# A table of parameters, gated opening loads, later spreads and a smaller GpSimd share in a hybrid decoder layer

## The chip, the core and the metric

The kernel runs on one core of a Trainium2 chip. The metric is the device time of one execution in microseconds (us). The engines named below are TensorE (PE, with its weight loads shown apart as PEld), VectorE (DVE), ScalarE (ACT), GpSimd (POOL) and SyncE (SP), whose queue issues all the transfers between HBM and the on-chip memory. The engines run side by side and wait for one another by semaphores.

## The reference

One layer of a decoder runs on 1024 prompt tokens and 8 sample tokens, 1032 columns in all, with a model width of 1024:

```python
h = rmsnorm(x, g_mix)
q, f, i, g, u = split(h @ w_in)              # 5 x 512 columns
y_a = hgrn2(silu(q), f, i) normed per head * hgrn_norm * sigmoid(g)
y_b = (pooled(u) @ pool_mix) * pool_scale    # windows 2, 4, 8, 16
x = x + concat(y_a, y_b) @ w_out
x = x + cross_attend(rmsnorm(x, g_cross), k, v, w_cq, w_co)   # k, v from rmsnorm(mem, g_mem) @ w_kv
x = x + (silu(a) * b) @ w_ffn_out            # a, b = split(rmsnorm(x, g_ffn) @ w_ffn_in)
y = rmsnorm(x, g_final)
```

It returns y, the recurrent states, the last pooling rows and the memory's keys and values, all in float32.

## The kernel before

Activations lie transposed, channels on the 128 partitions and the 1032 columns in three thirds of 344 (CH). Each float32 operand is split in a rounded high part and a low part, and a product is three matmuls per 128 rows of depth: high by high, low by high, high by low. A weight matrix is taken in stripes of 128 output channels, held in two slots. A stripe goes through SP's load into `raw`, ACT's rounding into `w_hi`, DVE's difference into `w_lo`, and then through three chunks on PE, one per third, each of 8 x 3 matmuls of 344 columns.

The opening is written out by hand. SP issues, in order, `g_mix` (L542), the first two stripes (L540), the nine parts of x that PE uses (L548; three parts a third, of 3, 3 and 2 of the 8 blocks of depth), and the nine blocks of token rows `xt` from which the norms are summed (L552), with stripe 2 behind the third and stripe 3 behind the last. Six small parameters follow (L557 to L567): the gains of the other norms, the bounds, `hgrn_norm` and `pool_scale`, each gathered in single elements. Only then stripes 4 and 5 are issued, and the states.

ACT rounds the first stripe in `first_hi(0)` (L1098, eight instructions), half of the second, three parts of x in `x_round` (L1112), the other half, and the remaining six parts. Then it squares the token rows (`x_square`, L1107) and makes the norm's factors of a third (`x_factors`). DVE makes the low parts: `first_lo(0)` (L1559), three times `x_rest` (L1552), `first_lo(1)`, six times `x_rest`. POOL makes constants first. PE waits for the ninth of them, runs seven warm-up products of 128 x 512 (L2293, `WARM`), and then `first_chunk` 0 to 5, which alternate between stripe 0 and stripe 1 over the thirds 0, 1 and 2. The second part of a chunk's x is needed at its fourth block of depth, the third part at its seventh.

The norm of x is applied when a chunk leaves PSUM. PE spreads the factors of a third over all partitions (`spread_rows`, L2269): third 0 after chunk 4, third 1 after chunk 5, third 2 after the first chunk of stripe 2. DVE copies the spread rows (L1566) and only then empties the chunks (`first_evac`, L1572; `plain_evac`, L1612).

Much later, at the mixer's end, y is gated (`gate`, L1757) and split. For the second third POOL makes four low parts (L901), DVE gates the last third, makes its four low parts (`rest_a`, L1798) and those of the pooled half (`rest_b`, L1804). PE enters the product with `w_out` and waits for these parts in `y_ready`.

Of the kernel before, what the change touches and what calls it, by code (L numbers as in the profile page):

```python
# [88 lines left out]
def hybrid_layer(nc, t):  # L89
# [9 lines left out]
    with ExitStack() as ctx:  # L99
# [29 lines left out]
        gains = put("gains", [P, 3, KB])  # L129
        gmem = put("gmem", [P, KB])  # L130
        lbt = put("lbt", [P, 2, H])
        lbw = put("lbw", [P, 4, H])
        omlb = put("omlb", [P, H])
        hnorm = put("hnorm", [P, H])
        pscale = put("pscale", [P, H])
# [126 lines left out]
        WARM = 7  # L262
# [18 lines left out]
        const_in = sem("const_in")  # L281
        gmix_in = sem("gmix_in")
# [238 lines left out]
        def _(sp):  # L521
            def load_stripe(p, i, s, wait=True):
# [19 lines left out]
            sp.dma_start(gains[:, 0, :], t["g_mix"].rearrange("(k p) -> p k", p=P),  # L542
                         allow_slow_non_contiguous=True).then_inc(gmix_in, 16)
# [12 lines left out]
            load_stripe(phases[0], 1, 1)  # L556
            sp.dma_start(gains[:, 1, :], t["g_cross"].rearrange("(k p) -> p k", p=P),  # L557
                         allow_slow_non_contiguous=True).then_inc(const_in, 16)
            sp.dma_start(gains[:, 2, :], t["g_ffn"].rearrange("(k p) -> p k", p=P),
                         allow_slow_non_contiguous=True).then_inc(const_in, 16)  # L560
            sp.dma_start(gmem[:, :], t["g_mem"].rearrange("(k p) -> p k", p=P),
                         allow_slow_non_contiguous=True).then_inc(const_in, 16)
            sp.dma_start(lbt[:, :, :], t["hgrn_lb"].rearrange("l (h p) -> p l h", p=P),
                         allow_slow_non_contiguous=True).then_inc(const_in, 16)
            sp.dma_start(hnorm[:, :], t["hgrn_norm"].rearrange("(h p) -> p h", p=P),
                         allow_slow_non_contiguous=True).then_inc(const_in, 16)
            sp.dma_start(pscale[:, :], t["pool_scale"].rearrange("(h p) -> p h", p=P),  # L567
                         allow_slow_non_contiguous=True).then_inc(const_in, 16)
# [231 lines left out]
        def _(pool):  # L800
# [87 lines left out]
            def mixer_end():  # L888
# [10 lines left out]
                for h in range(H):  # L899
# [118 lines left out]
            for p in phases:  # L1018
# [24 lines left out]
                if p is phases[0]:  # L1043
                    pool.wait_ge(gmix_in, 16)
# [30 lines left out]
        def _(act):  # L1075
# [17 lines left out]
            def first_hi(s, k0=0, k1=KB):  # L1093

                act.wait_ge(gmix_in, 16)
                act.wait_ge(raw_in[s], 16)
                for k in range(k0, k1):
                    last = act.activation(w_hi[s][:, k, :], raw[:, s, k, :], ACT.Copy, scale=gains[:, 0, k:k + 1])  # L1098
                if k1 == KB:
                    last.then_inc(hi_made, 1)  # L1100
# [431 lines left out]
        def _(dve):  # L1532
# [22 lines left out]
            def first_lo(s):  # L1555

                dve.wait_ge(hi_made, s + 1)
                for k in range(KB):
                    last = dve.scalar_tensor_tensor(w_lo[s][:, k, :], raw[:, s, k, :], gains[:, 0, k:k + 1],  # L1559
                                                    w_hi[s][:, k, :].bitcast(F32), ALU.mult, ALU.subtract)  # L1560
                last.then_inc(lo_made, 1)
# [681 lines left out]
        def _(pe):  # L2243
# [552 lines left out]
```

## Time and profile before

| | us |
|---|---|
| median of 3 runs | 1426.41 |
| lowest and highest | 1426.29, 1426.75 |
| the profiled execution, its own time | 1426.6 |
| its span, first to last instruction | 1424.8 |

The profiled execution spends 1.8 us outside its span. PE is busy for 1405.1 us of it. DVE is busy for 886.4, POOL for 576.4 and ACT for 420.5 us, so that PE is the engine whose idle time counts.

### The profile page before, as it was taken

Reading aid. Unit: us, or ns where it says so; the run is one execution under the profiler, and the core shown is the slowest. Engines: PE = TensorE matmul, PEld = TensorE weight load, DVE = VectorE, ACT = ScalarE, POOL = GpSimd, SP = SyncE. Lnnn points to the kernel's source line nnn. Section 1 sums busy time; section 2 is a strip of 40 time slices with the busy share of each in tenths; the row PEclk is TensorE's granted clock in tenths of the full one; section 3 lists DMA queues with packets and bytes.
Section 4 is the critical chain, followed back from the end, with each engine's and each line's share of the span. In section 5 each row is a group of like instructions: output and inputs, shape, how many; then the busy total and the mean of one; then the engine's idle time right before and its main releaser. Section 6 shows DMA issues by size and latency. Waiting matters only on the chain.

```text
span 1424.8 us, 25495 instructions
## 1 busy us (share of the span) xinstructions
PE 1405.1 (99%) x9965; PEld 1364.1 (96%) x9965; DVE 886.4 (62%) x1350; ACT 420.5 (30%) x632; POOL 576.4 (40%) x457
## 2 busy tenths in 40 slices
PE   9999999999999999999999999999999999999997
PEld 7999999989999988799999999999999999999996
DVE  4425677878754257757995676676667658633335
ACT  6131435370021136510052222323222222311111
POOL 1231246135532010134663787778777610000163
PEclk9999999999999999999999999999999999999999
DMA  9412211101162275611132222222222142523113
GB/s 297 127 45 67 68 31 38 38 23 46 50 185 61 74 251 173 212 45 45 44 89 75 76 74 89 74 70 78 89 74 67 54 155 74 173 93 109 33 45 119
DMA packets 163567, 129.19 MB, mean 91 GB/s; under 512 B 11532, under 2 KB 148748, under 8 KB 163363
## 3 DMA queue, kind: packets, MB, share of 16 engines
q1 hardware_dynamic: 163499, 128.25, 29.0%
q8 instruction: 47, 0.77, 0.2%
q14 instruction: 21, 0.17, 0.0%
HBM read 107.88 MB, written 20.58 MB: 90 GB/s over the span
## 4 chain that ended last, share of the span: by engine, by line
PE 67%; POOL 13%; issue 10%; DVE 7%; ACT 2%; POOLq 0%; DVEq 0%; ACTq 0%
PE pm L2249 17%; PE pm L2251 17%; PE pm L2250 17%; POOL raw L981 3%; POOL gb L999 3%; POOL raw_c L981 2%; POOL sum L988 2%; POOL sum L986 2%; PE pm L2520 2%; PE pm L2522 2%; PE pm L2521 2%; POOL raw_c L993 1%; POOL raw L993 1%; DVE xf L1826 1%; PE pm L2293 1%
## 5 line engine op out<-in xcount | busy, mean ns | idle before, releaser
L2249 PE MATMUL pm<-x_hi,w_hi 128*128 128x344 f32 x960 | 310.5, 323 | 0.6 <-DVE gb L1612 0.6
L2251 PE MATMUL pm<-x_hi,w_lo 128*128 128x344 f32 x960 | 306.6, 319 | 0.0
L2250 PE MATMUL pm<-x_lo,w_hi 128*128 128x344 f32 x960 | 306.6, 319 | 0.0
L1084 ACT ACTIVATE w_hi<-raw 128x1024 fp32r<-128x1024 f32 x88 | 93.3, 1060 | 530.2 <-PE pm L2251 444.7
L2249 PEld LDWEIGHTS pm<-x_hi,w_hi 128*128 128x128 f32 x960 | 180.5, 188 | 2.5 <-issue 1.8
L2250 PEld LDWEIGHTS pm<-x_lo,w_hi 128*128 128x128 f32 x960 | 180.4, 188 | 0.2
L2251 PEld LDWEIGHTS pm<-x_hi,w_lo 128*128 128x128 f32 x960 | 180.4, 188 | 0.0
L1545 DVE TENSOR_TENSOR w_lo<-raw,w_hi 128x1024 fp32r<-128x1024 f32 x79 | 113.8, 1441 | 9.7 <-ACT w_hi L1084 9.7
L831 POOL TENSOR_TENSOR raw<-raw,gains 128x1024 f32<-128x1024 f32 x32 | 64.7, 2025 | 127.4 <-DMA raw<-in_w_in 81.0
L2096 DVE TENSOR_TENSOR gb<-gb,ga 128x1032 f32<-128x1032 f32 x19 | 53.0, 2789 | 89.9 <-POOL gb L999 89.9
L2207 DVE TENSOR_TENSOR acc<-pm,acc 128x344 f32<-128x344 f32 x66 | 33.9, 516 | 112.1 <-PE pm L2251 112.0
L913 POOL TENSOR_TENSOR fp<-acc 128x344 f32 (+1 forms) x22 | 21.3, 967 | 201.8 <-DVE acc L2207 196.9
L998 POOL TENSOR_TENSOR ga<-ga,rb 128x1032 f32<-128x1032 f32 x19 | 52.6, 2769 | 85.9 <-DVE ga L2112 85.9
L2520 PE MATMUL pm<-x_hi,w_hi 128*128 128x258 f32 x304 | 86.6, 285 | 0.3
L2521 PE MATMUL pm<-tl,wh 128*128 128x258 f32 x304 | 85.9, 283 | 0.0
L2522 PE MATMUL pm<-th,wl 128*128 128x258 f32 x304 | 85.9, 282 | 0.0
L2520 PE MATMUL pm<-th,wh 128*128 128x258 f32 x304 | 85.8, 282 | 0.0
L2521 PE MATMUL pm<-tl,w_hi 128*128 128x258 f32 x304 | 85.8, 282 | 0.0
L2522 PE MATMUL pm<-x_hi,w_lo 128*128 128x258 f32 x304 | 85.7, 282 | 0.0
L2521 PE MATMUL pm<-x_lo,w_hi 128*128 128x258 f32 x304 | 85.7, 282 | 0.0
L2522 PE MATMUL pm<-th,w_lo 128*128 128x258 f32 x304 | 85.6, 282 | 0.0
L2520 PE MATMUL pm<-th,w_hi 128*128 128x258 f32 x304 | 85.6, 281 | 0.0
(366 smaller groups left out, 3972.9 us busy)
## 6 DMA issues: line engine op xcount, KB each, us to landing
raw<-in_w_ffn_in SPq DMA_DIRECT2D x24, 512.0 KB, 4.5
sg_raw<-s_rows SPq DMA_DIRECT2D x22, 516.0 KB, 5.0
s_rows<-gb SPq DMA_DIRECT2D x21, 516.0 KB, 2.7
raw<-in_w_in SPq DMA_DIRECT2D x20, 512.0 KB, 3.8
raw_c<-in_w_ffn_in SPq DMA_DIRECT2D x20, 512.0 KB, 5.0
sk<-in_cache_k_cols SPq DMA_DIRECT2D x16, 512.0 KB, 6.9
raw<-in_w_out SPq DMA_DIRECT2D x8, 512.0 KB, 3.6
raw<-in_w_cq SPq DMA_DIRECT2D x8, 512.0 KB, 3.6
```

The costliest lines, as they stand in the source:

```text
L831: pool.tensor_tensor(raw[:, s, :, :], raw[:, s, :, :], g, ALU.mult).then_inc(gain_on, 1)
L981: pool.tensor_tensor(r[:, s, :, :], r[:, s, :, :], g, ALU.mult).then_inc(gain7_on, 1)
L998: pool.tensor_tensor(ga[:, :], ga[:, :], rb[:, :], ALU.mult).then_inc(row_scaled, 1)
L1084: act.activation(w_hi[s][:, :, :], src, ACT.Copy).then_inc(hi_made, 1)
L1545: dve.tensor_tensor(w_lo[s][:, :, :], raw[:, s, :, :], w_hi[s][:, :, :].bitcast(F32), ALU.subtract).then_inc(lo_made, 1)
L2096: dve.tensor_tensor(gb[par][:, :], gb[par][:, :], ga[:, :], ALU.mult).then_inc(row_made, 1)
L2249: pe.matmul(out, w_hi[s][:, k, :], hi[:, k, x0:x0 + cols], start=(k == 0), stop=False)
L2250: pe.matmul(out, w_hi[s][:, k, :], lo[:, k, x0:x0 + cols], start=False, stop=False)
L2251: last = pe.matmul(out, w_lo[s][:, k, :], hi[:, k, x0:x0 + cols], start=False, stop=(k == kb - 1))
L2520: pe.matmul(out, wh7[n][:, j, :], hi(j, c), start=j == 0, stop=False)
L2521: pe.matmul(out, wh7[n][:, j, :], lo(j, c), start=False, stop=False)
L2522: last = pe.matmul(out, wl7[n][:, j, :], hi(j, c), start=False, stop=j == KP - 1)
```

## The change

It has five parts.

1. The seven small parameters are packed on the host into one array of 128 x 48 and loaded with one DMA into `table`, of which `gains`, `gmem`, `lbt`, `hnorm` and `pscale` become views. It takes the place of `g_mix` at the head of SP's queue.
2. Stripe 0 is loaded in two halves. SP holds the parts of x, stripe 1 and five of the blocks of token rows back until an earlier load has landed. Stripe 1 moves behind the third part of x and waits for the first part.
3. ACT and DVE make both stripes in halves, and PE starts its first chunk when the first half of stripe 0 and the first part of x are ready. ACT rounds the first half of stripe 1 ahead of the third part of x.
4. The warm-up becomes 20 products of 128 x 128 and waits for the third constant instead of the ninth. The spreads of the thirds 1 and 2 move one chunk later on PE, and ACT rounds stripe 2 ahead of three squares.
5. At the mixer's end POOL makes two of the four low parts of the second third, and DVE the other two ahead of its last gate.

```diff
-            sp.dma_start(gains[:, 0, :], t["g_mix"]...).then_inc(gmix_in, 16)
-            load_stripe(phases[0], 0, 0, False)
-            load_stripe(phases[0], 0, 1, False)
+            first_w = t["w_in"].rearrange("(k p) n -> p k n", p=P)[:, :, 4 * P:5 * P]
+            sp.dma_start(table[:, :], t["table"]).then_inc(table_in, 16)
+            sp.dma_start(raw[:, 0, 0:KP, :], first_w[:, 0:KP, :]).then_inc(first_in, 16)
+            sp.dma_start(raw[:, 0, KP:KB, :], first_w[:, KP:KB, :]).then_inc(raw_in[0], 16)
             for n in range(9):
                 c, (k0, k1) = n // 3, PARTS[n % 3]
+                if n == 1:
+                    sp.wait_ge(first_in, 16)
+                if n == 2:
+                    sp.wait_ge(raw_in[0], 16)
+                if n in (4, 5, 7, 8):
+                    sp.wait_ge(x_in[n - 3 if n < 6 else n - 4], 16)
+                if n == 6:
+                    sp.wait_ge(raw_in[1], 16)
                 sp.dma_start(xc[:, c, k0:k1, :], t["x_cols"][c, :, k0:k1, :]).then_inc(x_in[n], 16)
+                if n == 2:
+                    sp.wait_ge(x_in[0], 16)
+                    load_stripe(phases[0], 0, 1, False)
             for n in range(9):
...
+                if n < 3:
+                    sp.wait_ge(x_in[5 + n], 16)
+                if n == 4:
+                    sp.wait_ge(xt_in[0], 48)
+                if n == 7:
+                    sp.wait_ge(xt_in[1], 48)
                 sp.dma_start(xt[n][0:own, :], t["x_prompt"][0, t0:t0 + own, :]).then_inc(xt_in[n // 3], 16)
...
-            (six loads of small parameters)
...
-            first_hi(0)
-            first_hi(1, 0, KB // 2)
-            for n in range(3):
-                x_round(n)
-            first_hi(1, KB // 2, KB)
+            first_hi(0, 0, KP)
+            first_hi(0, KP, KB)
+            x_round(0)
+            x_round(1)
+            first_hi(1, 0, KP)
+            x_round(2)
+            first_hi(1, KP, KB)
...
             x_factors(0)
+            split_hi(phases[0], 1, 0, phases[0].done + 5)
             for n in range(3, 6):
                 x_square(n)
-            split_hi(phases[0], 1, 0, phases[0].done + 5)
...
-            pe.wait_ge(setup, 9)
+            pe.wait_ge(setup, 3)
             for _ in range(WARM):
-                pe.matmul(bank[7][:, :], ones[:, :], keep[:, :], start=True, stop=True)
+                pe.matmul(bank[7][:, 0:P], ones[:, :], ones[:, :], start=True, stop=True)
             for q in range(6):
                 first_chunk(q)
-                if q in (4, 5):
-                    spread_rows(q - 4)
+                if q == 4:
+                    spread_rows(0)
...
                 stripe_chunk(ph["qfi"], 1, 0, c, x_hi, x_lo)
-                if c == 0:
-                    spread_rows(2)
+                if c < 2:
+                    spread_rows(c + 1)
...
-                for h in range(H):
+                for h in range(2):
                     pool.wait_ge(yhi2_made, h + 1)
...
                 rest_b(1)
+                rest_a(1, 2)
                 gate(2)
-                rest_a(2)
+                rest_a(2, 0)
```

On SP, at the head of the program, these rows stood before, `xc` the parts of x and `raw` a stripe:

```order
1 L542 DMA gains<-in_g_mix 128x8x1
2 L540 DMA raw<-in_w_in 128x8x128 x2
3 L548 DMA xc<-in_x_cols 128x1032 x2
4 L548 DMA xc<-in_x_cols 128x688
5 L548 DMA xc<-in_x_cols 128x1032 x2
```

and these stand there now, with their waits (`first_in`, `raw_in0` and `raw_in1` are the halves of stripe 0 and stripe 1, `load_in0` and on the parts of x):

```order
1 L545 DMA table<-in_table 128x48
2 L546 DMA raw<-in_w_in 128x4x128
3 L547 DMA raw<-in_w_in 128x4x128
4 L558 DMA xc<-in_x_cols 128x1032
5 L558 DMA xc<-in_x_cols 128x1032 [waits first_in]
6 L558 DMA xc<-in_x_cols 128x688 [waits raw_in0]
7 L542 DMA raw<-in_w_in 128x8x128 [waits load_in0]
8 L558 DMA xc<-in_x_cols 128x1032
9 L558 DMA xc<-in_x_cols 128x1032 [waits load_in1]
```

Stripe 1 has moved from the third place in the queue to the seventh, and is issued after x's first part has landed.

On ACT, in the same stretch, before (`w_hi_52` is stripe 0, `w_hi_53` stripe 1):

```order
2 L1098 ACTIVATE w_hi_52<-raw,gains 128x128 x8
3 L1098 ACTIVATE w_hi_53<-raw,gains 128x128 x4
4 L1112 ACTIVATE x_hi<-xc 128x3x344 x2
5 L1112 ACTIVATE x_hi<-xc 128x2x344
6 L1098 ACTIVATE w_hi_53<-raw,gains 128x128 x4
```

and now:

```order
2 L1105 ACTIVATE w_hi_52<-raw,table 128x128 x8
3 L1118 ACTIVATE x_hi<-xc 128x3x344 x2
4 L1105 ACTIVATE w_hi_53<-raw,table 128x128 x4
5 L1118 ACTIVATE x_hi<-xc 128x2x344
6 L1105 ACTIVATE w_hi_53<-raw,table 128x128 x4
```

The first half of stripe 1 now stands between the second and the third part of x.

On DVE at the mixer's end, before:

```order
241 L1804 SCALAR_TENSOR_TENSOR y_lo<-pm,pscale,y_hi 128x344 [waits yb_hi] x4
242 L1757 TENSOR_TENSOR proj<-proj 128x344 [waits o_scaled,g_act]
243 L1757 TENSOR_TENSOR proj<-proj 128x344 [waits o_scaled] x3
244 L1798 TENSOR_TENSOR y_lo<-proj,y_hi 128x344 [waits yhi2_made] x4
245 L1804 SCALAR_TENSOR_TENSOR y_lo<-pm,pscale,y_hi 128x344 [waits yb_hi] x4
```

and now:

```order
245 L1815 SCALAR_TENSOR_TENSOR y_lo<-pm,table,y_hi 128x344 [waits yb_hi] x4
246 L1809 TENSOR_TENSOR y_lo<-proj,y_hi 128x344 [waits yhi2_made] x2
247 L1768 TENSOR_TENSOR proj<-proj 128x344 [waits o_scaled,g_act]
248 L1768 TENSOR_TENSOR proj<-proj 128x344 [waits o_scaled] x3
249 L1809 TENSOR_TENSOR y_lo<-proj,y_hi 128x344 [waits yhi2_made] x4
250 L1815 SCALAR_TENSOR_TENSOR y_lo<-pm,table,y_hi 128x344 [waits yb_hi] x4
```

Row 246 is new: two low parts of the second third stand ahead of the last third's gate.

## Rows read from the trace of the kernel before

**Rows 1.** The page, busy time: us, share of the span, instructions.

```profile
PE 1405.1 (99%) x9965; PEld 1364.1 (96%) x9965; DVE 886.4 (62%) x1350; ACT 420.5 (30%) x632; POOL 576.4 (40%) x457
```

**Rows 2.** Waits of PE, whole span: us in total, times, longest.

```profile
PE pm L2293 <- POOL eps L818: 3.4, 1, 3.4
PE pm L2355 <- DVE e L1682: 1.4, 1, 1.4
```

**Rows 3.** Timeline of PE and its weight loads, opening: start, us, what.

```profile
3.44 8.76 PE L2293 MATMUL pm<-keep,ones 128*128 128x512 f32 x14 [3.44 <-POOL eps L818]
11.82 0.54 PE L2283 MATMUL pm<-x_hi,w_hi 128*128 128x344 f32 x1
15.88 0.42 PE L2283 MATMUL pm<-x_hi,w_hi 128*128 128x344 f32 x1
7.87 0.34 PEld L2293 LDWEIGHTS pm<-keep,ones 128*128 128x128 f32 x1 [0.52 <-issue]
8.61 0.19 PEld L2293 LDWEIGHTS pm<-keep,ones 128*128 128x128 f32 x1 [0.40 <-issue]
```

**Rows 4.** Timeline of ACT, opening.

```profile
5.53 3.61 ACT L1098 ACTIVATE w_hi<-raw,gains 128x128 fp32r<-128x128 f32 x12 [3.43 <-DMA raw<-in_w_in]
10.61 1.73 ACT L1112 ACTIVATE x_hi<-xc 128x1032 fp32r<-128x1032 f32 x2 [0.20 <-DMA xc<-in_x_cols]
```

**Rows 5.** Timeline of DVE, opening.

```profile
10.44 3.28 DVE L1552 TENSOR_TENSOR x_lo<-xc,x_hi 128x1032 fp32r<-128x1032 f32 x3 [0.24 <-ACT x_hi L1112]
13.64 2.18 DVE L1559 SCALAR_TENSOR_TENSOR w_lo<-raw,gains,w_hi 128x128 fp32r<-128x128 f32 x8
```

**Rows 6.** Timeline of SP's queue: when it issued what.

```profile
1.30 1.19 SPq L540 DMA_DIRECT2D raw<-in_w_in  x2
2.53 5.47 SPq L548 DMA_DIRECT2D xc<-in_x_cols  x9
```

**Rows 7.** DMA issues in windows at 1.3, 1.95, 2.55 and 45: us to landing last.

```profile
raw<-in_w_in SPq DMA_DIRECT2D x1, 512.0 KB, 4.1
raw<-in_w_in SPq DMA_DIRECT2D x1, 512.0 KB, 5.2
xc<-in_x_cols SPq DMA_DIRECT2D x1, 516.0 KB, 6.8
raw<-in_w_in SPq DMA_DIRECT2D x1, 512.0 KB, 3.8
```

**Rows 8.** Timeline of PE and DVE and ACT around the third spread.

```profile
39.43 0.21 ACT L1119 ACTIVATE rtok<-rtok 128x3 f32<-128x3 f32 x1
40.32 0.80 PE L2269 MATMUL pm<-ident,rtok 128*128 128x128 f32 x6
41.15 0.52 DVE L1566 COPY rb<-pm 128x344 f32<-128x344 f32 x1 [3.13 <-PE pm L2269]
42.98 2.44 DVE L1545 TENSOR_TENSOR w_lo<-raw,w_hi 128x1024 fp32r<-128x1024 f32 x1
35.15 1.23 DVE L1545 TENSOR_TENSOR w_lo<-raw,w_hi 128x1024 fp32r<-128x1024 f32 x1 [1.76 <-ACT w_hi L1084]
```

**Rows 9.** Timeline at the mixer's end: DVE, POOL, PE.

```profile
312.80 3.23 DVE L1757 TENSOR_TENSOR proj<-proj 128x344 f32<-128x344 f32 x4
317.66 2.01 DVE L1804 SCALAR_TENSOR_TENSOR y_lo<-pm,pscale,y_hi 128x344 fp32r<-128x344 f32 x4
311.09 4.14 POOL L901 TENSOR_TENSOR y_lo<-proj,y_hi 128x344 fp32r<-128x344 f32 x4 [8.20 <-ACT y_hi L1250]
315.33 0.40 PE L2249 MATMUL pm<-y_hi,w_hi 128*128 128x344 f32 x1 [0.24 <-issue]
319.73 0.42 PE L2249 MATMUL pm<-y_hi,w_hi 128*128 128x344 f32 x1 [0.38 <-DVE y_lo L1804]
302.45 2.10 DVE L1757 TENSOR_TENSOR proj<-proj 128x344 f32<-128x344 f32 x4
315.95 1.79 DVE L1798 TENSOR_TENSOR y_lo<-proj,y_hi 128x344 fp32r<-128x344 f32 x4
```

More of the change, by code:

```diff
@@ L128, in hybrid_layer @@
         rb = put("rb", [P, T])
-        gains = put("gains", [P, 3, KB])
-        gmem = put("gmem", [P, KB])
-        lbt = put("lbt", [P, 2, H])
+        table = put("table", [P, 48])
+        gains = table[:, 0:3 * KB].rearrange("p (n k) -> p n k", n=3)
+        gmem = table[:, 24:32]
+        lbt = table[:, 32:40].rearrange("p (n h) -> p n h", n=2)
+        hnorm, pscale = table[:, 40:44], table[:, 44:48]
         lbw = put("lbw", [P, 4, H])
         omlb = put("omlb", [P, H])
-        hnorm = put("hnorm", [P, H])
-        pscale = put("pscale", [P, H])
         ss = put("ss", [P, 16])
@@ L1093, in first_hi @@
             def first_hi(s, k0=0, k1=KB):
-                act.wait_ge(gmix_in, 16)
-                act.wait_ge(raw_in[s], 16)
+                act.wait_ge(table_in, 16)
+                act.wait_ge(*((first_in, 16) if (s, k0) == (0, 0) else (raw_in[s], 16)))
                 for k in range(k0, k1):
                     last = act.activation(w_hi[s][:, k, :], raw[:, s, k, :], ACT.Copy, scale=gains[:, 0, k:k + 1])
-                if k1 == KB:
-                    last.then_inc(hi_made, 1)
+                last.then_inc(*((hi_made, 1) if k1 == KB else (first_halves, 1)))
             def x_square(n):
@@ L1553, in x_rest, with first_lo @@
                                   ALU.subtract).then_inc(x_split, 1)
-            def first_lo(s):
-                dve.wait_ge(hi_made, s + 1)
-                for k in range(KB):
+            def first_lo(s, k0, k1):
+                dve.wait_ge(table_in, 16)
+                dve.wait_ge(*((hi_made, s + 1) if k1 == KB else (first_halves, s + 1)))
+                for k in range(k0, k1):
                     last = dve.scalar_tensor_tensor(w_lo[s][:, k, :], raw[:, s, k, :], gains[:, 0, k:k + 1],
                                                     w_hi[s][:, k, :].bitcast(F32), ALU.mult, ALU.subtract)
-                last.then_inc(lo_made, 1)
+                last.then_inc(*((lo_made, 1) if k1 == KB else (first_rests, 1)))
             def spread_factors(c):
@@ L1794, in mixer_end, with rest_a @@
             def mixer_end():
-                def rest_a(c):
-                    for h in range(H):
+                def rest_a(c, h0):
+                    for h in range(h0, H):
                         dve.wait_ge(yhi2_made, H * (c - 1) + h + 1)
@@ L2275, in first_chunk @@
                 s, c = FIRST_CHUNKS[q]
-                pe.wait_ge(lo_made, s + 1)
+                pe.wait_ge(*((first_rests, s + 1) if c == 0 else (lo_made, s + 1)))
                 out, at = bank[q][:, 0:CH], slice(c * CH, (c + 1) * CH)
@@ L2471, in y_ready @@
                 pe.wait_ge(yb_made, H * (c + 1))
-                pe.wait_ge(*((ya2_made, H) if c == 2 else (ya_made, H * (c + 1))))
+                if c < 2:
+                    pe.wait_ge(ya_made, (H, H + 2)[c])
+                if c:
+                    pe.wait_ge(ya2_made, (None, 2, 2 + H)[c])
             def norm_sums(n):
@@ L2788 @@
     t["cache_k_cols"] = nc.dram_tensor("in_cache_k_cols", a.shape, mybir.dt.from_np(a.dtype), kind="ExternalInput").ap()
+    g = [inputs[n].reshape(KB, P).T for n in ("g_mix", "g_cross", "g_ffn", "g_mem")]
+    g += [inputs[n].reshape(-1, P).T for n in ("hgrn_lb", "hgrn_norm", "pool_scale")]
+    arrays["in_table"] = a = np.ascontiguousarray(np.concatenate(g, axis=1))
+    t["table"] = nc.dram_tensor("in_table", a.shape, mybir.dt.from_np(a.dtype), kind="ExternalInput").ap()
     t["s_rows"] = nc.dram_tensor("s_rows", (P, FB, T), F32).ap()
```

34 lines of the change are left out of this document (13 added, 21 removed).

## The prediction

> **What bounds the kernel now.** I read the busy times first. PE works for 1405.1 of the span's 1424.8 us [rows 1], so the kernel gains only where PE stands idle or does work that computes nothing, and loses where an edit makes PE wait. The list of PE's waits shows where that is: 3.4 us before its first warm-up product, 1.4 us in the recurrence and little else [rows 2]. The timeline of the opening shows the large piece. PE starts at 3.44 us with seven warm-up products, 14 records of 8.76 us in all, and its first useful matmul starts at 11.82 us [rows 3]. All 11.8 us are without use, and from then on PE has hardly a gap: the second chunk starts at 15.88 [rows 3], as DVE's low part of stripe 1, 2.18 us from 13.64 on, ends [rows 5].
>
> Who holds the first matmul? ACT rounds stripe 0 and half of stripe 1 in 3.61 us from 5.53 on [rows 4]. Then it waits for the first part of x, which SP issued at 2.53 [rows 6] and which landed 6.8 us later, at 9.3 [rows 7]. With 1.06 us of rounding and one of DVE's three parts, begun at 10.44, x is ready about 11.5 [rows 5], and the warm-up ends at 11.6 or so. Both end together.
>
> **The opening, step by step.** Times are from the span's start, with before's durations.
>
> The table takes g_mix's place, and stripe 0 is issued at 1.3 us as before. Its first half is half the bytes of a load that took 4.1 us from issue [rows 7]. I take 4.3 for its landing and 5.2 for the whole stripe. ACT's eight rounding instructions take 0.3 us each (3.61 for twelve, [rows 4]), so they run from 4.4 to 6.8. DVE's take 0.27 us each (2.18 for eight, [rows 5]), and its second half ends at 7.9.
>
> The first part of x is now the second half megabyte in the queue. In the trace before that was stripe 1, issued at 1.9 and landed after 5.2 us, at 7.1 [rows 6, 7]. I take 6.8 for x. Its rounding ends at 7.9 and its low part at 9.0. The first useful matmul can start at 9.1, some 2.7 us sooner, if the warm-up is over.
>
> The warm-up starts when POOL's third constant is set, between 0 and the 3.4 us at which before's nine and two more were there [rows 2]; I take 1.8. Forty passes of 128 columns by the fast level of the trace, some 0.13 us each (0.80 for six, [rows 8]), would be over at 7; by twice that they would be over at 12.4. The level changes on the way: the weight loads of the old warm-up took 0.34 us up to 7.87 and 0.19 from 8.61 on, 1.2 GHz and then 2.4 [rows 3], some 5 us after PE began. With 5 us of the slow level from 1.8 on, that is 19 passes, and 21 fast ones in 2.7 us, PE is free at 9.5. If the level changed no sooner than 8.5 it is free at 10.1. Either start turns out not to matter.
>
> It is the next link that decides. SP sends stripe 1 only when x's first part is there, at 6.9 instead of 1.9. A load of a stripe took 3.8 us from issue in a calm place and 5.2 behind another [rows 7]. I take 4.2, nearer to the calm place because at most three loads are under way, and so 11.1. On ACT the first half of stripe 1 stands ahead of x's third part. So from 11.1 on: half a stripe on ACT 1.2 us (four times 0.3), the third part of x 0.72 (what is left of 1.73 after a first of 1.0, [rows 4]), its low part on DVE 0.85 (0.8 to 1.1, a share of 3.28 for three, [rows 5]), and the first half of stripe 1's low part 1.1 (half of 2.18, [rows 5]), with 0.2 us of handing over. The sum is 4.1 us, and chunk 1 can start at 15.2 instead of 15.88. Meanwhile PE has done six of the eight blocks of chunk 0 by 13.1 at the latest, stops there for the third part of x until 14.1, does two blocks in 1.0 us, and stops again for 0.1. So of the 2.7 us that the start wins, two are given back within the first chunk, and **0.7 us** stays. Were stripe 1 to take 3.8 us, 1.1 us would stay; at 5.2 the loss would be 0.3.
>
> The Trainium skill, in "DMA: Bandwidth & Descriptors", section "Anatomy of one DMA — SWDGE (gpsimd) path", puts a fixed cost of some 2.0 us on each DMA and its bytes over 436 GB/s on top of that. That speaks against loads that are sent one after another's landing, and this trace agrees in kind, with 3.8 us for 512 KB in a calm place [rows 7]. By the page's figures, an estimate for another path than SP's, stripe 1 would take 3.2 us and land at 10.1, and 1.7 us would stay.
>
> After chunk 1 nothing in the opening should fall behind. Six more parts of x take ACT about 5.5 us from 14.3 on, and DVE as long; chunk 2 needs its first at 19 us. The loads of x were all issued by 8.0 before and arrived in line; now up to three or four are in flight, and I count nothing for their gaps, which chunk 2's late need covers.
>
> **The later spreads.** They cost PE nothing: the same 18 records move. Their factors were there at 39.6, 0.7 us ahead of the third spread [rows 8], and the spread now comes 3.8 us later, so stripe 2's rounding may stand ahead of three squares. What becomes late next is the other side. DVE copies the third spread, empties chunks 4 and 5 and one of stripe 2, and starts stripe 3's low part 1.83 us after the copy began (41.15 to 42.98, [rows 8]). That low part takes 1.23 us alone and 2.44 beside a POOL product [rows 8]. Before it had two chunks of time, now it has one of 3.8 us: 3.1 us of work fits, 4.3 would stop PE for 0.5. The POOL product beside it was stripe 4's gain. Stripe 4 is issued once stripe 2's low part is made. That now comes ahead of three squares, and no small loads stand in stripe 4's way, so POOL should be done with it before DVE comes to stripe 3. I expect no meeting, and take zero, with 0.5 us lost as the other bound.
>
> **The six small loads** lie beside other work: no wait of PE hangs on them. Removing them costs and gains nothing but that room in the queue.
>
> **The mixer's end.** PE starts the second third at 315.33, 0.24 us late, when POOL's fourth low part is ready, and the last third at 319.73, 0.38 us late, for DVE [rows 9]. Two low parts fewer on POOL end it near 313.2, so the first wait goes. DVE gets two low parts more, 0.45 us each (1.79 for four), but its gate, 3.23 us for four beside POOL, falls to 2.10 as where POOL is idle [rows 9]. That is +0.9 and -1.1: DVE is done 0.2 us sooner at best, and the last third waits for DVE in any case. So the 0.24 us saved first is mostly waited for second. I take **0.1 us** of gain, from 0.3 lost (the gate as slow as before) to 0.4 won.
>
> **The sum.** 0.7 and 0.1 make 0.8 us less. The profiled execution would go from 1426.6 to 1425.8, and the median from 1426.41 to 1425.6. I put the forecast there. Where PE's other waits follow its own progress, they move along with it and give nothing back.
>
> **The rivals.**
>
> *The loads come as the change would like them.* Fewer in flight means less mixing, and x's first part lands at 6.2 and stripe 1 after 3.5 us more, at 9.8. Then chunk 1 starts at 13.9 and 2.0 us are won, with the mixer 2.2: 1424.2. For it: the loads in the old opening took up to 6.8 us with nine parts of x behind them, 3.8 elsewhere [rows 7]. Against it: no load of that size took under 3.8.
>
> *Slower: stripe 1 mixes with the parts of x.* It is issued with parts 4 and 5 right behind it, as the first part of x was before, and that one took 6.8 us [rows 7]. Then it lands at 13.7, chunk 1 starts at 17.8, and 1.9 us are lost: 1428.3 with nothing from the mixer. It decides from a landing at 11.8 on (15.88 less 4.1). Against it: the first two stripes, with x behind them, took only 4.1 and 5.2.
>
> *The clock falls back.* PE now stands still twice in chunk 0. Were it to run the first chunks at 1.2 GHz, each chunk would take 3.8 us more; one such chunk makes 1428.5 or so. Against it: PE also stood still 1.4 us in the recurrence [rows 2].
>
> *The later spread stops PE* for 0.5 us beside POOL: 1426.1.
>
> **How the numbers follow.** Forecast and its neighbourhood (0 to 1.5 us won) 0.58, early loads 0.18, late stripe 0.12, clock 0.04, spread 0.08. The likeliest is 1425.6. The range holds the early loads and the first part of the late ones: 1424.0 to 1427.2. A change of 0.2%, 2.85 us, is about what can be told from none. All of PE's useless time before 11.82 that could vanish is 2.7 us, so faster by more takes both ends at once: 0.07. Slower by more needs the late stripe at its worst, or the clock: 0.05. The rest, 0.88, is no change.
>
> **What would show it.** The first useful matmul at 9 to 10 us and the start of the second chunk near 15.2 (right), at 14 (early loads), past 15.9 (late). ACT idle ahead of stripe 1's first half, released by its load, near 11.1. No wait ahead of stripe 3's first matmul. At the mixer's end no wait for POOL, and one of 0.4 to 0.6 us for DVE ahead of the last third. The forecast is wrong if chunk 1's start moves by over 1.5 us, or if PE loses time in a place that is not named here.

## The result, and the profile after

The changed kernel takes 1428.8 us in the median of 22 executions (1426.47 to 1430.85), the kernel before 1426.5 (1425.9 to 1429.9). The ratio of the two is 1.0014, with a 95% interval of 1.0008 to 1.0019: 2.0 us more, between 1.1 and 2.7 (the medians differ by 2.3). By the median that lies within the 0.2% that the prediction calls no change, but the interval lies wholly on the slower side, and 1428.8 is outside the predicted range. The forecast was 1425.6. The profiled execution of the changed kernel, at 1430.75, is one of its slower ones: its span is 1428.9 us against 1424.8 [rows 1]. So its trace shows about twice the typical loss.

PE's longest waits after the change (us in total, times, longest), against [rows 2]:

```profile
PE pm L2297 <- DVE x_lo L1560: 5.3, 2, 3.3
PE pm L2307 <- POOL ones L812: 1.8, 1, 1.8
PE pm L2369 <- DVE e L1693: 1.4, 1, 1.4
```

There are two stops inside the opening that were not there. The timeline of PE (start, length, what, and in brackets the idle time ahead with what ended it) answers to [rows 3]:

```profile
1.75 6.23 PE L2307 MATMUL pm<-ones 128*128 128x128 f32 x40 [1.75 <-POOL ones L812]
9.99 0.39 PE L2297 MATMUL pm<-x_hi,w_hi 128*128 128x344 f32 x1 [2.01 <-DVE x_lo L1560]
...
12.75 0.32 PE L2299 MATMUL pm<-x_hi,w_lo 128*128 128x344 f32 x1
16.38 0.65 PE L2297 MATMUL pm<-x_hi,w_hi 128*128 128x344 f32 x1 [3.31 <-DVE x_lo L1560]
16.82 0.49 PE L2298 MATMUL pm<-x_lo,w_hi 128*128 128x344 f32 x1
...
18.26 0.49 PE L2297 MATMUL pm<-x_hi,w_hi 128*128 128x344 f32 x1
...
21.98 0.33 PE L2298 MATMUL pm<-x_lo,w_hi 128*128 128x344 f32 x1
...
23.72 0.32 PE L2297 MATMUL pm<-x_hi,w_hi 128*128 128x344 f32 x1
```

The warm-up ends at 8.0. Chunk 0 starts at 9.99, 1.8 us sooner than before, runs six blocks, and stands still until 16.38. Chunk 1 starts at 18.26 instead of 15.88 [rows 3], and chunk 2 at 23.72, 4.0 us later than the 19.75 of the trace before. Behind the second stop a matmul takes 0.49 us where it took 0.32. The view by windows (window, its length, busy time and count of PE, PEld, DVE, ACT and POOL, granted clock, DMA share, GB/s) says why:

```profile
8.00:12.00 4.00, 2.01 (x13) 2.03 (x14) 3.07 (x5) 1.64 (x2) 0.00 (x0) 1.00 0.87 288
12.00:16.00 4.00, 1.07 (x7) 0.78 (x5) 0.56 (x1) 2.53 (x8) 0.00 (x0) 0.89 0.99 359
16.00:20.00 4.00, 3.62 (x13) 3.63 (x14) 4.00 (x11) 4.00 (x6) 0.00 (x0) 0.50 0.92 307
20.00:24.00 4.00, 4.00 (x21) 4.00 (x21) 4.00 (x5) 1.74 (x3) 0.00 (x0) 0.75 0.98 316
```

From 15.2 to 22.0 us the clock is granted at 0.50, which is 1.2 GHz. In the trace before it stays at 1.00 from chunk 0 on. The fall comes 2.1 us after the last of the six blocks has ended, while PE stands still.

Behind the second stop stands ACT, whose rows answer to [rows 4]:

```profile
8.99 1.06 ACT L1118 ACTIVATE x_hi<-xc 128x1032 fp32r<-128x1032 f32 x1 [0.41 <-DMA xc<-in_x_cols]
13.47 1.28 ACT L1105 ACTIVATE w_hi<-raw,table 128x128 fp32r<-128x128 f32 x4 [3.41 <-DMA raw<-in_w_in]
14.65 0.76 ACT L1118 ACTIVATE x_hi<-xc 128x688 fp32r<-128x688 f32 x1
```

DVE follows, against [rows 5]:

```profile
15.44 0.88 DVE L1560 TENSOR_TENSOR x_lo<-xc,x_hi 128x688 fp32r<-128x688 f32 x1 [4.12 <-ACT x_hi L1118]
16.23 2.19 DVE L1568 SCALAR_TENSOR_TENSOR w_lo<-raw,table,w_hi 128x128 fp32r<-128x128 f32 x8
```

and SP's queue, against [rows 6]:

```profile
2.27 4.08 SPq L558 DMA_DIRECT2D xc<-in_x_cols  x3
7.51 0.38 SPq L542 DMA_DIRECT2D raw<-in_w_in  x1
7.93 8.39 SPq L558 DMA_DIRECT2D xc<-in_x_cols  x6
```

The landing of stripe 1 and of the part of x issued right behind it, against [rows 7] (KB, us to landing):

```profile
raw<-in_w_in SPq DMA_DIRECT2D x1, 512.0 KB, 5.9
xc<-in_x_cols SPq DMA_DIRECT2D x1, 516.0 KB, 6.8
```

Read together: stripe 1 is issued at 7.51 and lands 5.9 us later, at 13.4. ACT stood idle for it, with the third part of x, landed since about 10, queued behind. PE needs that third part for the last two blocks of chunk 0.

The 4.0 us by which chunk 2 is late can be divided. Before the stop, with the clock at 1.00, matmuls start 0.16 us apart, so from 16.38 chunk 1 would have started at 17.3: the stop costs 1.4 us. From 16.38 to 21.98 there are 19 of them, 5.6 us where 3.0 would do: the clock costs 2.6 us.

The spreads cost nothing, as the timeline of DVE at stripe 3 shows, against [rows 8]. The low part takes 1.22 us, alone:

```profile
48.53 0.52 DVE L1575 COPY rb<-pm 128x344 f32<-128x344 f32 x1 [2.95 <-PE pm L2281]
...
50.37 1.22 DVE L1553 TENSOR_TENSOR w_lo<-raw,w_hi 128x1024 fp32r<-128x1024 f32 x1
```

The mixer's end, against [rows 9], POOL, DVE and PE each from their own timeline:

```profile
314.64 1.82 POOL L908 TENSOR_TENSOR y_lo<-proj,y_hi 128x344 fp32r<-128x344 f32 x2 [8.19 <-ACT y_hi L1258]
```

```profile
316.35 0.93 DVE L1809 TENSOR_TENSOR y_lo<-proj,y_hi 128x344 fp32r<-128x344 f32 x2
317.21 1.79 DVE L1768 TENSOR_TENSOR proj<-proj 128x344 f32<-128x344 f32 x4
```

```profile
312.13 0.58 PE L2261 MATMUL pm<-y_hi,w_hi 128*128 128x344 f32 x1
...
318.22 0.58 PE L2261 MATMUL pm<-y_hi,w_hi 128*128 128x344 f32 x1
...
322.69 0.43 PE L2261 MATMUL pm<-y_hi,w_hi 128*128 128x344 f32 x1 [0.29 <-DVE y_lo L1815]
```

The second third starts 6.09 us after the first. Before, it took from 308.58 to 315.33 [rows 9], 6.75. From first to last third it is 10.56 us, before 11.15: 0.6 us won. In both traces DVE's last low part is what the last third waits for.

### The profile page after: what moved, and what is told of

Its sections match the earlier page's. It is cut to its first block, busy times and chain, and to the rows that moved or that the text cites. A ratio compares the mean times of both kernels' runs of the same rounds, so it can differ in the third digit from the quotient of the medians.

```text
span 1428.9 us, 25548 instructions
## 1 busy us (share of the span) xinstructions
PE 1405.5 (98%) x9991; PEld 1369.6 (96%) x9991; DVE 882.4 (62%) x1352; ACT 420.8 (29%) x632; POOL 576.5 (40%) x455
## 4 chain that ended last, share of the span: by engine, by line
PE 88%; DVE 7%; ACT 2%; DMA 1%; issue 1%; POOL 1%; SPq 0%; POOLq 0%; DVEq 0%; ACTq 0%
PE pm L2261 17%; PE pm L2263 17%; PE pm L2262 17%; PE pm L2537 9%; PE pm L2539 9%; PE pm L2538 9%; DVE w_lo L1553 1%; DVE xf L1838 1%; DVE acc L2177 1%; PE pm L2297 1%; PE pm L2396 1%; PE pm L2605 1%; PE pm L2299 1%; PE pm L2298 1%; PE pm L2639 1%
## 5 line engine op out<-in xcount | busy, mean ns | idle before, releaser
L838 POOL TENSOR_TENSOR raw<-raw,table 128x1024 f32<-128x1024 f32 x32 | 64.7, 2026 | 131.4 <-DMA raw<-in_w_in 84.7
```

The lines of the kernel that those rows point to most:

```text
L838: pool.tensor_tensor(raw[:, s, :, :], raw[:, s, :, :], g, ALU.mult).then_inc(gain_on, 1)
```

## The experiments

The theory after this reading: the loss comes from stripe 1, issued late and landing late, and from the clock that falls because PE stands still. The rivals: the waits of SP as such, the later spreads, the small table, the mixer's end. The experiments were made in three groups of four: fill, early, nogates and mixer; shortwarm, earlywarm, thirdwarm and spreads; table, nogateswarm, mixer_again and best2. Each is compared with executions of the kernel before that were made with its group. These took 1426.63, 1427.62 and 1426.36 us in the median, and none of 33, 10 of 35 and 3 of 33 took over 1429.5. So the second group's kernel before is a slower yardstick. The ratios given are those on record and need not equal the ratio of two medians.

**fill** keeps everything and gives PE work in its second stop, 12 products that nobody reads.

```diff
                 for k in range(KB):
+                    if q == 0 and k == 6:
+                        for _ in range(FILL):
+                            pe.matmul(bank[7][:, 0:P], ones[:, :], ones[:, :], start=True, stop=True)
```

> The changed kernel, with twelve more idle products of 128 x 128 on PE ahead of the seventh block of chunk 0, where PE stood still from 12.9 to 16.4 us and the clock then showed 0.50 from 15 to 22 us. Theory 1 (the clock fell because PE stood still, and that is half of the loss or more): the filler takes about 3 us inside the stop and delays nothing, no LDWEIGHTS of 0.33 us is seen after 12 us, chunk 1 is done 2 to 3.4 us sooner than in the profiled run of the change, and the time is 1426 to 1427.5, near the kernel before or 1 us above. Theory 2 (only the late stripe matters, the clock is a by-product that runs through anyway): the time stays at the change's 1428.8.

Measured: 1427.52 us, ratio 1.0006 [0.9997, 1.0015]. The windows show the clock at 1.00 and PE busy throughout the second:

```profile
8.00:12.00 4.00, 2.13 (x12) 1.81 (x12) 2.56 (x3) 1.42 (x2) 0.00 (x0) 1.00 0.84 273
12.00:16.00 4.00, 4.00 (x35) 4.00 (x34) 1.21 (x3) 3.19 (x10) 0.00 (x0) 1.00 0.94 338
```

The clock did not fall, though PE had stood still for 1.7 us ahead of chunk 0. Chunk 1 started at 16.77, which is 0.9 us late instead of 2.4. The kernel gains 1.3 us on the changed one by the medians, 1.1 by the two ratios to the kernel before, whose intervals overlap a little. What is left is 0.9 us. In its profile, whose span is 1.3 us longer than before's, chunk 1's delay has shrunk to 0.4 when the mixer's product with `w_out` starts, the new mixer's end wins 0.6, and the attention takes 1.4 us longer, of which more below.

**early** issues stripe 1 right behind stripe 0, as before, and keeps the other waits of SP. **nogates** is the same without any of the new waits.

```diff
             sp.dma_start(raw[:, 0, KP:KB, :], first_w[:, KP:KB, :]).then_inc(raw_in[0], 16)
+            load_stripe(phases[0], 0, 1, False)
...
-                if n == 2:
-                    sp.wait_ge(x_in[0], 16)
-                    load_stripe(phases[0], 0, 1, False)
```

> The changed kernel, with stripe 1 issued right behind stripe 0 and ahead of x instead of behind x's third part; all other gates kept. Theory 1 (the late stripe 1 costs the time): stripe 1 lands near 7 us, x's first part near 9, chunk 0 starts near 11 and runs through, chunk 1 starts at about 15, the clock does not fall, and the time is 1425 to 1426.5, 2 to 3 us below the change. Theory 2 (the gates themselves lose it, wherever stripe 1 stands): chunk 1 no sooner than 16.5, time 1427.5 or more.

> The changed kernel with all of SP's new waits in the opening taken out and stripe 1 right behind stripe 0, so that loads are issued as before the change (table, halves, ACT's order, warm-up, spreads and mixer's end as changed). Theory 1 (gating gains nothing, or costs): the same time as with stripe 1 early and the gates kept, or less, 1425 to 1426.5. Theory 2 (gates do bring x sooner, the place of stripe 1 was the only fault): 0.5 to 1.5 us slower than the run with gates and stripe 1 early, as x's first part lands at 9.3 instead of 8.5.

Measured: 1428.27 us, ratio 1.0009 [1.0000, 1.0018], and 1428.32 us, ratio 1.0011 [1.0002, 1.0020]. Here x lands late, chunk 0 starts at 12.20 and 12.46, and the only stop is the one between the warm-up's end and chunk 0. PE's timeline in the first of the two, and its window:

```profile
1.75 6.26 PE L2305 MATMUL pm<-ones 128*128 128x128 f32 x40 [1.75 <-POOL ones L810]
12.20 0.63 PE L2295 MATMUL pm<-x_hi,w_hi 128*128 128x344 f32 x1 [4.18 <-DVE x_lo L1558]
12.62 0.49 PE L2296 MATMUL pm<-x_lo,w_hi 128*128 128x344 f32 x1
```

```profile
12.00:16.00 4.00, 3.80 (x15) 3.83 (x16) 3.37 (x8) 4.00 (x12) 0.00 (x0) 0.59 0.91 293
```

The clock falls in both, and both miss the 1425 to 1426.5 us of their first theory. With the old order of loads the new kernel is still slower (early's interval just reaches nothing, that of nogates does not), so the late stripe is not the whole cause: the warm-up, which here ends at 8.0 and 8.4, opens the same door by itself. Not all of this loss is the clock's. The mixer's product with `w_out` starts 1.0 and 1.4 us late in the two profiles, the new mixer's end wins 0.6 back, and the attention takes 1.4 and 1.1 us longer than in the trace before.

**mixer** is the kernel before with the mixer's end alone (PE's waits in `y_ready` are changed to match).

```diff
-                for h in range(H):
+                for h in range(2):
                     pool.wait_ge(yhi2_made, h + 1)
...
+                rest_a(1, 2)
                 gate(2)
-                rest_a(2)
+                rest_a(2, 0)
```

> The kernel before with the mixer's end alone changed (POOL two low parts, DVE the other two). By the prediction 0.1 us faster, 0.3 lost to 0.4 won. By the trace of the change, where the distance from the product's first matmul to the last third's start fell from 11.15 to 10.59 us, 0.5 us faster. Either is 1425.9 to 1426.4.

Measured: 1426.08 us, ratio 0.9994 [0.9985, 1.0003]. From first to last third 10.57 us, where before has 11.15 and two other kernels with the old end 11.15 and 11.14.

**shortwarm** is the kernel before with the new warm-up alone, 20 products of 128 columns from the third constant on.

```diff
-        WARM = 7
+        WARM = 20
...
-            pe.wait_ge(setup, 9)
+            pe.wait_ge(setup, 3)
             for _ in range(WARM):
-                pe.matmul(bank[7][:, :], ones[:, :], keep[:, :], start=True, stop=True)
+                pe.matmul(bank[7][:, 0:P], ones[:, :], ones[:, :], start=True, stop=True)
```

> The kernel before with the warm-up alone changed (20 products of 128 x 128 from the third constant on). Theory 1 (the warm-up that ends near 8 us lets the clock fall while PE waits for x until 11.8): the first useful matmul stays near 11.8, the clock shows 0.50 for some us after 12, chunk 1 starts 1 to 2 us later than 15.88, and the time is 1 to 2 us above before, 1427.5 to 1428.5. Theory 2 (only the late stripe stops PE long enough): the clock does not fall, same time as before, 1426.6.

Measured: 1428.23 us, ratio 1.0009 [0.9997, 1.0021]. The windows and PE's timeline:

```profile
12.00:16.00 4.00, 4.00 (x18) 4.00 (x17) 4.00 (x11) 3.95 (x9) 0.00 (x0) 0.60 1.02 412
```

```profile
11.61 0.48 PE L2283 MATMUL pm<-x_hi,w_hi 128*128 128x344 f32 x1 [3.62 <-DVE x_lo L1552]
...
318.71 0.41 PE L2249 MATMUL pm<-y_hi,w_hi 128*128 128x344 f32 x1 [2.97 <-DVE y_lo L1804]
```

Chunk 0 starts when it did before, after a stop of 3.6 us, and then runs at 1.2 GHz. Chunk 1 starts at 16.99, 1.1 us late. This one edit brings the fall of the clock that I had argued away. The time alone does not prove it, as its interval reaches nothing. Its twelve executions lie in two groups, seven between 1427.3 and 1428.3 and five between 1431.3 and 1433.9. The profiled one, one of the five, has a stop of 3 us at the old mixer's end too. The row's bracket names DVE, but it is POOL's fourth low part that ends last, at 318.6. POOL's row is this, against the 4.14 of [rows 9]:

```profile
311.75 6.87 POOL L901 TENSOR_TENSOR y_lo<-proj,y_hi 128x344 fp32r<-128x344 f32 x4 [8.19 <-ACT y_hi L1250]
```

and DVE's gate beside it was not held up at all, against 3.23:

```profile
313.47 1.79 DVE L1757 TENSOR_TENSOR proj<-proj 128x344 f32<-128x344 f32 x4
```

**earlywarm** and **nogateswarm** are early and nogates with a warm-up that lasts until x is there.

```diff
-        WARM = 20
+        WARM = 36
```

> The changed kernel with stripe 1 issued right behind stripe 0 (gates kept) and 36 warm-up products instead of 20, so that PE works until about 12 us. Theory 1 (late stripe and fallen clock are all that the opening loses): the clock does not fall, chunk 0 starts near 12.2 and chunk 1 near 16.0 instead of 17.44, and the time is 1426.0 to 1426.7. Theory 2 (the gates lose something further on, on x's later parts): chunks 2 to 5 show stops, or the time stays at 1427.5 or more.

> All of the change, but SP's new waits left out, stripe 1 right behind stripe 0, and 36 warm-up products. Against the same with the gates kept (1427.04 in another job, chunk 1 at 15.68) this shows what the gates do by themselves. Theory 1 (a gate only delays an issue, the bytes flow at the same rate): chunk 1 within 0.4 us of 15.7 and the same time. Theory 2 (gates bring the first part sooner): chunk 1 at 16.0 or later. No clock fall in either.

Measured: 1427.04 us, ratio 0.9991 [0.9982, 1.0000], and 1426.92 us, ratio 1.0001 [0.9992, 1.0010]. The warm-ups end at 11.7 and 11.9, the stop ahead of chunk 0 is 0.2 and 0.4 us, the clock stays at 1.00, and chunk 1 starts at 15.68 and 16.12. By the medians they are 1.2 and 1.4 us faster than early and nogates, which differ from them in the length of the warm-up alone, though they were made in other groups; in the profiles the mixer's product starts 1.6 and 1.7 us sooner. Against their own kernels before, early and nogates were 1.6 and 1.7 us slower, these 0.6 faster and 0.6 slower. Whether SP waits or not is worth 0.4 us of chunk 1's start, and nothing that the times can tell.

The mean granted clock is on record for every execution, not for the profiled ones alone. Averaged over a kernel's executions it is 0.9977 or 0.9978 in fill, earlywarm, nogateswarm, thirdwarm and best2, and 0.9977 in the kernel before in two of the three groups. In early it is 0.9966, in nogates 0.9962, in the changed kernel 0.9969, and 0.9969 in shortwarm too, with the falls at its mixer's end. So the fall is no accident of one profile, and a warm-up that lasts takes it away. An estimate from these means: 0.0008 of 1428 us, at half the full clock, is 2.3 us spent at 1.2 GHz in the average execution of the changed kernel, a third of the 6.8 us in its profile. At that profile's price of 2.6 us for 6.8, it costs about 0.9 us.

**thirdwarm** rounds the third part of x ahead of stripe 1, issues stripe 1 without a wait behind that part, has no other wait of SP, and 30 products.

```diff
-        WARM = 20
+        WARM = 30
...
             x_round(1)
-            first_hi(1, 0, KP)
             x_round(2)
+            first_hi(1, 0, KP)
```

> A version meant to beat both: table, halves, later spreads and mixer's end as changed; no gates; x's first third issued ahead of stripe 1 and rounded on ACT ahead of it; 30 warm-up products. If loads land by their order in the queue: x's third part by 10.5, stripe 1 by 12, chunk 0 starts near 10.7, chunk 1 at 14.5 to 15.3, clock does not fall, time 1424.7 to 1426. If loads in flight mix whatever their order: stripe 1 lands at 13 or later, chunk 1 at 16.5, and the time is 1427 or more.

Measured: 1426.83 us, ratio 0.9993 [0.9984, 1.0001]. Chunk 0 starts at 11.26 and chunk 1 at 15.34. Stripe 1, with all of x in flight, took 8.9 us to land:

```profile
raw<-in_w_in SPq DMA_DIRECT2D x1, 512.0 KB, 8.9
```

The opening did nearly what was hoped and the time did not follow: 1424.7 to 1426 was expected. PE comes to the attention 1.8 us sooner than in the trace before, and has lost all of it when the attention ends.

**spreads** is the kernel before with the later spreads, and ACT's rounding of stripe 2 ahead of three squares.

```diff
-                if q in (4, 5):
-                    spread_rows(q - 4)
+                if q == 4:
+                    spread_rows(0)
...
-                if c == 0:
-                    spread_rows(2)
+                if c < 2:
+                    spread_rows(c + 1)
```

> The kernel before with the spreads of the thirds 1 and 2 a chunk later and ACT's rounding of stripe 2 ahead of three squares, nothing else. The prediction: no cost and no gain, unless stripe 3's low part meets a POOL product, then 0.5 us. Stripe 2's first chunk may start 0.1 to 0.4 us sooner, as its low part was ready only with it (36.38). Time 1426.2 to 1426.7.

Measured: 1426.45 us, ratio 0.9997 [0.9986, 1.0008]: nothing. From chunk 1 to the first product of stripe 3 it takes 32.3 us, before 32.7.

**table** is the kernel before with one table in place of the seven small loads.

```diff
-            sp.dma_start(gains[:, 0, :], t["g_mix"]...).then_inc(gmix_in, 16)
+            sp.dma_start(table[:, :], t["table"]).then_inc(table_in, 16)
...
-            (six loads of small parameters)
```

> The kernel before with the one table in place of the seven small loads, nothing else. The prediction: no wait of PE hangs on them, same time as before within 0.3 us. Rival (the 4-byte packets of g_mix at the queue's head keep some DMA engines behind the others, so that x's first part landed late at 9.3): x's first part lands 0.5 us or more sooner, yet PE still starts when the old warm-up ends, 11.6 to 11.8, and the time falls by 0.2 at most.

Measured: 1427.17 us, ratio 1.0008 [0.9999, 1.0017]. In its profile the first part of x lands 5.9 us after its issue at 2.35, so at 8.3 and not 9.3, and chunk 1 starts at 15.30, 0.6 us sooner than in the trace before and 0.3 sooner than in mixer_again, whose opening is that of before:

```profile
xc<-in_x_cols SPq DMA_DIRECT2D x1, 516.0 KB, 5.9
```

The span is 1424.8 all the same. Why the median is 0.8 us higher stays open; the interval reaches nothing. Two of its eleven executions lie above 1430, as executions of the old mixer's end do.

**mixer_again** is mixer once more, to see whether the gain and the absence of long executions hold.

> The kernel before with the mixer's end alone changed, a second time. In one profile of a kernel with the old mixer's end GpSimd's four low parts took 6.9 us instead of 4.1, PE stood still for 3.0 us and the clock fell after it; single runs 3 to 5 us above the rest were seen in kernels with the old end only. Theory 1 (the old end has this stop now and then, the new one hardly): no run of this kernel over 1428.5, while some of the kernel before are. Theory 2 (those runs have another cause): both kernels show them alike. Median 0.3 to 0.6 us below before.

Measured: 1425.81 us, ratio 0.9997 [0.9988, 1.0006]. First to last third 10.56 us. The median is 0.55 us below before's, as it was the first time, and neither interval excludes nothing. One execution of eleven took 1430.75. It has no profile, so I can't say that the new end never stops PE.

**best2** tries to take all that was learned: 29 products, stripe 1 issued right behind the third part of x, later parts held back so that they don't mix with it, and the third part rounded first.

```diff
-                if n in (4, 5, 7, 8):
-                    sp.wait_ge(x_in[n - 3 if n < 6 else n - 4], 16)
-                if n == 6:
+                if n == 3:
+                    sp.wait_ge(x_in[1], 16)
+                if n == 4:
+                    sp.wait_ge(x_in[2], 16)
+                if n == 5:
                     sp.wait_ge(raw_in[1], 16)
...
                 if n == 2:
-                    sp.wait_ge(x_in[0], 16)
                     load_stripe(phases[0], 0, 1, False)
```

> A version meant to beat both kernels: the change, with x's first third and stripe 1 issued without waiting for x's first part, the parts of the second third held back until x's second and third part and stripe 1 have landed, the third part of x rounded ahead of stripe 1 on ACT, and 29 warm-up products. Theory 1 (stripe 1 is late in the change because it waits and then shares the engines with the parts behind it): x's first part lands at 7 to 7.5, stripe 1 at 11 to 11.8, chunk 0 starts near 10 and runs through, chunk 1 at 14 to 14.8, the clock stays up, and the time is 1 to 2 us below the kernel before. Theory 2 (stripes land late whatever is behind them): stripe 1 at 12.5 or later, chunk 1 no sooner than 15.3.

Measured: 1426.45 us, ratio 0.9997 [0.9988, 1.0006]. The opening works: chunk 0 at 10.78, chunk 1 at 14.64, 1.2 us sooner than before, the clock at 1.00. Its stripe 1, issued at 5.50 with no other load issued for 3.1 us behind it, still took 6.3 us, with three parts of x under way ahead of it. Then PE waits at the first spread, twice as long as at a spread in any other trace here:

```profile
PE pm L2284 <- ACT rtok L1128: 1.2, 1, 1.2
```

The spread needs the squares of the token rows, and ACT's timeline shows them late:

```profile
26.80 1.06 ACT L1116 ACTIVATE junk<-xt 128x1024 f32<-128x1024 f32 x1 [5.17 <-DMA xt<-in_x_prompt]
```

In the trace before, the same row starts at 22.16. The waits that keep the parts of x apart keep the token rows back as well. The spread starts at 31.05, where it started at 31.07. So the opening's whole gain went into this wait. What the later spreads and the mixer's end win is still there at the start of the attention, which comes 1.2 us sooner than before, and is lost in the attention, which takes 1.0 us longer. No version that I ran beats both kernels clear of noise.

## Why the prediction was wrong

**The failed step** is this sentence: "I take 4.2, nearer to the calm place because at most three loads are under way, and so 11.1." Stripe 1 took 5.9 us. Two parts of x were still landing when it was issued, and three more were issued before it landed, at 7.93, 8.98 and 9.84, the first of them taking 6.8. The rival of the late stripe had it so: it put the landing at 13.7. Whether the loads ahead or the loads behind held stripe 1 up stays open, as best2's took 6.3 us with none behind it for 3.1 us. It was also issued 0.6 us later than I had it, since x's first part landed at 7.5 and not 6.8. From 11.1 to 13.4 makes 2.3 us. The chain behind the landing was right: I gave 4.1 us to chunk 1, and without the clock it is 3.9. Chunk 1 would have started at 17.3, against the rival's 17.8, and been 1.4 us late where I had it 0.7 early. I had the rows for both cases, 3.8 and 6.8 [rows 7], and gave the mixed one 0.12.

**The second failure** is "Either start turns out not to matter", said of the warm-up's end, and with it the dismissal of the clock. I asked of the warm-up only whether it delays chunk 0. It also bridges the time until x is there. It ended at 8.0, not at 9.5 or 10.1, because its weight loads, 0.33 us each at first, took 0.19 from 5.0 on, and not from 6.8 or 8.5, and because its slow passes started 0.21 us apart and not 0.26. (My 10.1 was also added up wrongly: a change at 8.5 gives 10.3.) Chunk 0's start, 9.99, was as predicted, but it left 2.0 us idle ahead, and the stop in chunk 0 became 3.3 us instead of one. My evidence against a fall was a single stop of 1.4 us [rows 2], and it says nothing of longer ones: shortwarm falls after 3.6 us, early after 4.2, the changed kernel in the second of two stops, of 2.0 and 3.3 us with 3.1 us of work between, while fill, after 1.7 us ahead of chunk 0, and best2, after 1.2 us at the spread, do not. The clock rival had 0.04, and its price was off: with starts 0.29 instead of 0.16 us apart a chunk of 24 costs 3.1 us more and not 3.8, and 3.8 on top of 1425.6 is 1429.4 and not 1428.5. In the profiled execution it costs more, 2.6 us, than the stripe; fill puts it at 1.1 to 1.3 us of the typical execution, and the estimate from the mean clocks at 0.9.

So the two rivals that I priced apart, 1.9 us for the stripe and 3.8 for a chunk at the slow clock, are one chain in the changed kernel: the early end of the warm-up and the late stripe make the stops in which the clock falls. Their joint case had no place in the range.

**The spreads** were right: no meeting with POOL, no stop at stripe 3, and nothing in spreads' time. **The small loads** were half right. No wait hangs on the six. But in table the first part of x lands 1.0 us sooner and chunk 1 starts 0.6 sooner. The six come behind x in the queue, so this comes from the exchange at its head, the table for the single elements of `g_mix`, for which I had counted nothing. About 0.2 us of it is that x was issued sooner, at 2.35 instead of 2.53.

**The mixer's end** went the right way and was mis-sized: 0.1 us predicted, 0.6 measured between starts in the three traces of the new end quoted above, outside my bounds of −0.3 and +0.4. In the medians, 0.55 us twice, it is not clear of noise. The mis-sized term is the gate: beside an idle POOL it fell to 1.79 us and not to 2.10. With that, DVE is done with its last low part 0.6 us sooner after the first third's start, two more low parts included, and the last third waits for DVE. The wait for POOL was off as well, though the total does not hang on it: I took it from its bracket, 0.24 us [rows 9], but the start of the second third moved by 0.66, as the mixing products' row ahead, with a modelled end, covered part of the idle time.

The Trainium skill, in "DMA: Bandwidth & Descriptors", section "Anatomy of one DMA — SWDGE (gpsimd) path", would have had stripe 1 take 3.2 us by its figures, an estimate for another path. This trace gives 5.9 and thirdwarm 8.9. The page's form has a fixed cost and the bytes, and no term for other loads under way; 2.7 us of the one and 5.7 of the other are not in it.

**A place that I had not named** lost time too. In the sum for the profiled execution, 1.4 for the stop and 2.6 for the clock, less 0.6 at the mixer's end, is 3.4 of the span's 4.1. The stretch of the attention adds 1.0, and small gains elsewhere take 0.3 off. From the first product of the memory's values to the first product with `w_co` it takes 89.7 us in the trace before (524.25 to 613.97) and 90.7 in the changed kernel. It takes 90.7 to 91.5 in all the seven other profiles with the changed opening or a variant of it (fill, early, nogates, earlywarm, nogateswarm, thirdwarm, best2), 89.7 in spreads and mixer_again, 90.0 in table, 90.2 in mixer, and 91.0 in shortwarm. Eight of eight is hardly chance, but shortwarm, which has only the new warm-up, shows it too. In shortwarm and in seven of the eight, one wait of PE is new, 0.4 to 1.1 us for a load of the cached values (`vc_b`). The load lands 67.0 to 67.8 us into the stretch, in the trace before at 65.6, and PE goes on within 0.2 us of it. In fill there are waits for `sk` and for `vc_a` instead. Why that load is issued later, I did not find out, and made no run for it. So the openings of earlywarm, nogateswarm, thirdwarm and best2 had won 1.1 to 1.8 us when PE came to this stretch, and 0.2 at most was left behind it.

For the typical execution of the changed kernel these add up, as an estimate, to 0.9 to 1.4 us for the stripe, 0.9 for the clock and 1.0 in the attention, less 0.6 at the mixer's end: 2.2 to 2.7, where 2.0 to 2.3 was measured.

## What to carry to other kernels

A warm-up has two ends to check: it must not delay the first real product, and it must last until that product can run. Price a load that you move by rows of loads that had others under way on both sides of them, not by a row from a calm place, and look at what stands behind it in the order of the engine that takes it. Where one rival's delay is another rival's cause, give the two together a chance and a place in the range; and take the cost of a wait from the distance between starts, not from the idle time in brackets. A gain in the opening is worth only what is left of it at the end, so follow it through the later stages.

## What the runs showed of the hardware

The granted clock came down to 1.2 GHz in the opening of four kernels, each time in or just after the stops named above, and stayed there for 3.4 us (early, nogates, shortwarm) or 6.8 us (the changed kernel). Chunk 1 was late by 1.1 to 2.4 us in these. The record of the granted clock does not tell everything about pace: it reads 1.00 through both warm-ups, although the weight loads take 0.33 or 0.34 us at first and 0.19 later, and 0.33 and 0.19 are their times at 0.50 and at 1.00 in chunks 0 to 1 of the changed kernel.

One load of 512 KB took from 3.8 us in a calm place [rows 7] to 5.9 us (the changed kernel), 6.3 (best2) and 8.9 (thirdwarm) in an opening with other loads under way, in which the DMA share was 0.87 to 1.05 in windows of 4 us.

Beside each other, POOL's four low parts and DVE's gate of four had two outcomes in traces of the same code. Either DVE is held up (3.23 us, with POOL at 4.14 [rows 9]), or POOL is (6.87 us, with DVE at 1.79). In the second case PE waits 3 us more and the clock falls once more, from 319.0 to 322.4. The Trainium skill, "SBUF — State Buffer", section "SBUF: two separate sides", calls the port pair that the two share an exclusive lock, which the loser waits for in full. The rows agree with that in kind: POOL's two low parts alone take 1.82 us, so four would take 3.64, and the 3.2 us more are about what DVE's gate and its low parts beside it take, from 313.5 to 317.0. Which of the two wins is not fixed by the code of this stretch, which is the same in both. The executions of the old end above 1429.5 us may be these; only one of them has a profile.
